# An encoder layer in fp32 on one core: x transposed ahead of the modulation rows, and g1, sh2, sc2 summed on VectorE during the projections

## The chip, the cores and the metric

The kernel runs on one core of a Trainium2 chip. The metric is the time of one execution on the device, in microseconds (us). TensorE multiplies matrices, VectorE and ScalarE work on elements and read its results out of PSUM, GpSimd is a slower helper, SyncE issues most of the loads. The profile calls them PE, DVE, ACT, POOL and SP.

## The reference

One layer (512 tokens, width 1024), then a mixture of experts. The parts that the change touches are the modulation and what comes before and around the four input projections:

```python
c_act = jax.nn.silu(c)
mod = (c_act @ w_mod[l] + b_mod[l])[:, None, :]
sh1, sc1, g1, sh2, sc2, g2 = jnp.split(mod, 6, axis=-1)
h = rms_norm(x) * (1.0 + sc1) + sh1
z = h @ w_in[l]
u_pool, q, k, v, g, r_f, r_b = jnp.split(z, split_at, axis=-1)
y_pool = pool_mixer(u_pool, w_pool[l], pool_scale[l])
y_gla = gla_mixer(q, k, v, g, r_f, r_b, w_gk_up[l], b_gk[l], gla_norm_g[l])
mix = jnp.concatenate([y_pool, y_gla], axis=-1) @ w_out[l]
x = x + g1 * mix
h = rms_norm(x) * (1.0 + sc2) + sh2
x = x + g2 * moe_ffn(h, w_router, b_router, w1[l], w3[l], w2[l])
return rms_norm(x) * final_g
```

c is one row of 1024 numbers, w_mod is 1024 x 6144, so mod is one row of 6144 numbers and costs a read of 25 MB. The result is float32; the projections are computed as three products of high and low parts.

## The kernel before

Everything is written out by hand: each engine has its own program, and they meet at semaphores. The order of the code is the order on each engine.

**Loads.** The ring has 8 slots of 2 MB. Until the experts begin, SyncE uses slots 0 to 3 in turn (STREAM): m0 to m3, u, qk, v, g, m4 to m11, wo0, wo1. "m" units are 512 columns of w_mod, u, qk, v, g those of w_in, wo those of w_out. Each load waits until the slot's last unit is used up. Slots 6 and 7 hold scratch (scr) in this phase: q, k, v, the pooling input `up`, the rows of the first modulation numbers (modr).

**TensorE's jobs.** JOBS is the list of results in PSUM, in TensorE's order. Job number j takes bank j % 8, and start() makes TensorE wait until job j - 8 has been read out, by ScalarE (OUT_SCALAR) or VectorE (OUT_VECTOR), each in its own order.

**Modulation.** mod_rows(i) multiplies c, spread to 32 columns (cb), by the unit m_i in four column groups of the array: 8 products (line 532), each in two instructions. For m0 to m3 (sh1, sc1) ScalarE copies the result (mr0 to mr3) to modr, and 16 small products with `sel` (line 545) turn it into columns (mcol), to which VectorE adds the bias (modc). For m4 to m11 (g1, sh2, sc2, g2) mod_pair spreads the row over all partitions by a product with `sel` (line 635, jobs mb4 to mb11), and VectorE adds a bias that GpSimd loads as a broadcast over 128 partitions (bias_b, line 1684, issued after g3).

**Start.** ScalarE sums squares of x, VectorE makes xn, and TensorE, after mcol, transposes it in 32 transposes (line 551, xT0 to xT7). ScalarE scales and shifts each (line 1074), VectorE splits it in h_hi and h_lo.

**Projections.** product() runs over 8 chunks k of a unit; for each, ScalarE writes w_hi (line 1067), VectorE w_lo (line 1297), in DEPTH = 4 buffers, and TensorE does 12 products (line 572). The order is u, r (low_rank), q and k, gk (line 619), v, yp (line 625, the pooling's map), g. Meanwhile GpSimd does the pooling windows of u (lines 1674 to 1681), ScalarE and VectorE the gates: from gk comes the negative absolute value (neg_abs), then exp, ln (softplus), then a scan over each chunk (lines 1321 to 1325). Their place in VectorE's program is fixed between low_weights(20, 24) and low_weights(24, 28).

**Attention and output.** After g: the decays on ScalarE (line 1116), decayed(i) on VectorE (lines 1338 to 1341), the products att, the mask copies (line 1375), the transposes kdt, the products upd, the states (lines 1392 and 1395), the products o (lines 686 and 698), and the output projection wo0, wo1 with the norms. Then the second norm, the router, and 16 pairs of experts.

Of the kernel before, what the change touches and what calls it, by code (L numbers as in the profile page):

```python
# [25 lines left out]
F32 = mybir.dt.float32  # L26
# [7 lines left out]
P = 128  # L34
D = 1024
S = 512
# [31 lines left out]
CP = dict(ident=(0, 128), iota=(128, 192), off=(192, 200), tok=(200, 204))  # L68
CP_N = 204
# [19 lines left out]
def constants():  # L89
# [6 lines left out]
    cp[:, 200:204] = r[:, None] + P * np.arange(NT)[None] - S  # L96
    ct = np.zeros((P, CT_N), np.float32)
# [11 lines left out]
    for w, (_, _, ed) in zip(WINDOWS, POOL_AT):  # L109
# [9 lines left out]
JOBS = ([f"mr{i}" for i in range(4)] + ["mcol"] + [f"xT{k}" for k in range(KD)]  # L119
        + [f"u{i}" for i in range(4)] + ["r", "q0", "q1", "k0", "k1"] + [f"gk{i}" for i in range(4)]  # L120
        + [f"v{i}" for i in range(4)] + [f"yp{i}" for i in range(4)] + [f"g{i}" for i in range(4)]
        + [f"m{a}{i + j}" for i in (4, 6) for a in "rb" for j in range(2)]
        + [f"att{d}{h}" for d in range(2) for h in range(HEADS)]
        + [f"kdt{d}{p}" for d in range(2) for p in range(2)]
        + [f"m{a}{8 + j}" for a in "rb" for j in range(2)]
        + [f"upd{d}{p}{par}" for d in range(2) for p in range(2) for par in range(2)]
        + [f"m{a}{10 + j}" for a in "rb" for j in range(2)]
# [6 lines left out]
STREAM = (["m0", "m1", "m2", "m3", "u", "qk", "v", "g"] + [f"m{i}" for i in range(4, 12)] + ["wo0", "wo1"])  # L134
SU = {n: i for i, n in enumerate(STREAM)}
PRE_UNITS = len(STREAM)
# [5 lines left out]
OUT_SCALAR = ([f"mr{i}" for i in range(4)] + [f"xT{k}" for k in range(KD)]  # L142
              + [f"u{i}" for i in range(4)] + ["r", "q0", "q1", "k0", "k1"] + [f"gk{i}" for i in range(4)]
              + [f"yp{i}" for i in range(4)] + [f"g{i}" for i in range(4)]
              + [f"mr{i}" for i in range(4, 8)]
              + [f"kdt{d}{p}" for d in range(2) for p in range(2)]
              + [f"mr{i}" for i in range(8, 12)] + [f"o{h}" for h in range(HEADS)]
              + [f"hT{t}{hf}" for t in range(NT) for hf in range(2)] + ["lg"])
OUT_VECTOR = (["mcol"] + [f"v{i}" for i in range(4)] + [f"mb{i}" for i in range(4, 8)]
              + [f"att{d}{h}" for d in range(2) for h in range(HEADS)] + ["mb8", "mb9"]  # L150
              + [f"upd{d}{p}{par}" for d in range(2) for p in range(2) for par in range(2)]
              + ["mb10", "mb11"] + [f"rb{h}" for h in range(HEADS)]
# [3 lines left out]
PRE_USES = [len(range(i, PRE_UNITS, PRE_SLOTS)) if i < PRE_SLOTS else 0 for i in range(SLOTS)]  # L156


def build(nc, A, out, g2_row, x1_row):
    ctx = ExitStack()  # L160
    with ctx:
# [29 lines left out]
        h_hi = place("h_hi", BIG, [P, KD, S], F32R)  # L191
# [172 lines left out]
        def unit(slot, k):  # L364
            return ring[:, slot, :].rearrange("p (k n) -> p k n", k=k)
# [68 lines left out]
        def _(sp):  # L434
# [4 lines left out]
            for n in range(PRE_UNITS):  # L439
                slot = n % PRE_SLOTS  # L440
                if n >= PRE_SLOTS:
                    used_up(sp, n - PRE_SLOTS)
# [1301 lines left out]
```

## Time and profile before

| what | value |
|---|---|
| median of 3 runs | 794.06 us (788.34, 796.72, 794.06) |
| profiled execution | 791.07 us, span 789.2 us |
| TensorE busy, share of the span | 706.9 us, 90% |
| VectorE busy | 300.2 us, 38% |
| ScalarE busy | 175.5 us, 22% |
| GpSimd busy | 46.6 us, 6% |
| mean granted TensorE clock | 0.950 of full speed |
| end of the first output projection's second half (wo13) | 244.6 us |

The span runs from the first to the last instruction; 1.9 us lie around it. The work named above fills the first 245 us; the router and the experts fill the rest.

### The profile page before, as it was taken

The numbers are of one execution on the slowest core, as the hardware profiler recorded it, in microseconds if no ns is written. First come the engines' busy times: TensorE is split into PE (matmuls) and PEld (weight loads), VectorE is DVE, ScalarE is ACT, GpSimd is POOL, SyncE is SP. The second block draws the span as 40 slices with busy tenths as digits, with TensorE's granted clock in tenths as the row PEclk, the third lists the DMA queues.
The fourth block names the chain that finished last, engine by engine and source line by source line (L and its number), as shares of the span: only waits on it lengthen the run. The fifth ranks groups of instructions, "written<-read, shape, count | busy, mean of one in ns | idle before, by whom it ended". The sixth has DMA issues, their size and how long they took to land.

```text
span 789.2 us, 9101 instructions
## 1 busy us (share of the span) xinstructions
PE 706.9 (90%) x3786; PEld 382.4 (48%) x3786; DVE 300.2 (38%) x565; ACT 175.5 (22%) x308; POOL 46.6 (6%) x50
## 2 busy tenths in 40 slices
PE   1899999989998289999877999999999998998994
PEld 0388787457686234443333434434443453453442
DVE  1081354177685602333304233333333333322326
ACT  3153363514335012101110101102111110110104
POOL 0004700000000000000000000000000000000000
PEclk9789999999999579999986999999999999999998
DMA  9983330797226939999997799999999999999972
GB/s 338 387 321 108 107 106 6 299 387 285 92 108 229 425 123 432 424 429 397 426 417 310 289 404 428 428 426 423 429 428 425 426 425 429 426 427 426 427 312 106
DMA packets 38857, 261.22 MB, mean 331 GB/s; under 512 B 4002, under 2 KB 4386, under 8 KB 26016
## 3 DMA queue, kind: packets, MB, share of 16 engines
q1 hardware_dynamic: 34560, 250.64, 77.4%
q0 software_dynamic: 2480, 6.16, 2.1%
q10 hardware_dynamic: 1776, 3.84, 1.3%
q8 instruction: 31, 0.51, 0.3%
q14 instruction: 10, 0.08, 0.0%
HBM read 260.76 MB, written 4.20 MB: 336 GB/s over the span
## 4 chain that ended last, share of the span: by engine, by line
PE 73%; DMA 19%; DVE 5%; ACT 2%; issue 1%; SPq 1%; DVEq 0%; ACTq 0%; POOLq 0%
PE bank L841 23%; PE bank L572 17%; DMA ring<-in_w 12%; PE bank L850 12%; PE bank L858 3%; PE bank L859 2%; DMA x_rows<-mid 2%; PE bank L532 2%; DMA ring<-in_w_mod 2%; PE bank L815 2%; PE bank L830 1%; DVE x L1549 1%; DMA xg_rows<-x_rows,keep 1%; DMA after<-in_b_mod 1%; PE bank L833 1%
## 5 line engine op out<-in xcount | busy, mean ns | idle before, releaser
L841 PE MATMUL bank<-ring,low 128*64 128x512 f32 x1024 | 230.0, 603 | 12.3 <-DMA ring<-in_w 9.7
L841 PEld LDWEIGHTS bank<-ring,low 128*64 128x64 f32 x1024 | 77.2, 139 | 155.3 <-issue 155.3
L1549 DVE TENSOR_TENSOR x<-x,bank 128x512 f32<-128x512 f32 x136 | 84.4, 682 | 84.5 <-PE bank L859 82.7
L850 PE MATMUL bank<-ring,low 128*64 128x512 f32 x512 | 113.4, 595 | 0.9 <-DVE x L1549 0.9
L850 PEld LDWEIGHTS bank<-ring,low 128*64 128x64 f32 x512 | 36.2, 137 | 66.1 <-issue 64.4
L1539 DVE SCALAR_TENSOR_TENSOR y_raw<-bank,keep,g2b 128x512 f32<-128x512 f32 x32 | 24.0, 751 | 88.4 <-PE bank L850 88.4
L858 PE MATMUL bank<-y_hi,slot_tok 128*128 128x512 f32 x128 | 53.8, 420 | 0.2 <-DVE y_lo L1544 0.2
L1599 DVE TENSOR_TENSOR low<-low,bank 128x512 f32<-128x512 f32 x16 | 11.0, 689 | 112.7 <-PE bank L841 112.7
L859 PE MATMUL bank<-y_lo,slot_tok 128*128 128x512 f32 x128 | 50.6, 395 | 0.0
L1228 ACT COPY low<-bank 128x512 f32<-128x512 f32 x16 | 9.4, 586 | 175.8 <-PE bank L823 175.8
L532 PE MATMUL bank<-ring,low 128*32 128x512 f32 x192 | 28.6, 737 | 18.0 <-DMA ring<-in_w_mod 17.8
L1236 ACT CAST y_hi<-y_raw 128x512 fp32r<-128x512 f32 x32 | 19.8, 618 | 105.5 <-DVE y_raw L1539 105.5
L1699 POOL DMA_INDIRECT xg_rows<-x_rows,keep x16 | 15.9, 997 | 441.4 <-PE bank L815 396.4
L1297 DVE TENSOR_TENSOR w_lo<-ring,w_hi 128x512 fp32r<-128x512 f32 x32 | 22.9, 727 | 45.7 <-ACT w_hi L1067 45.7
L858 PEld LDWEIGHTS bank<-y_hi,slot_tok 128*128 128x128 f32 x128 | 24.0, 187 | 30.0 <-issue 25.2
L572 PE MATMUL bank<-h_hi,w_hi 128*128 128x512 f32 x96 | 37.9, 394 | 0.0
L572 PE MATMUL bank<-h_hi,w_lo 128*128 128x512 f32 x96 | 37.4, 390 | 0.0
L572 PE MATMUL bank<-h_lo,w_hi 128*128 128x512 f32 x96 | 37.4, 390 | 0.0
L1226 ACT ACTIVATE low<-bank 128x512 f32<-128x512 f32 x16 | 9.6, 597 | 101.1 <-PE bank L841 101.1
L1544 DVE TENSOR_TENSOR y_lo<-y_raw,y_hi 128x512 fp32r<-128x512 f32 x32 | 22.2, 693 | 21.9 <-ACT y_hi L1236 21.9
L1067 ACT CAST w_hi<-ring 128x512 fp32r<-128x512 f32 x32 | 19.7, 619 | 46.4 <-PE bank L572 46.4
L859 PEld LDWEIGHTS bank<-y_lo,slot_tok 128*128 128x128 f32 x128 | 24.1, 188 | 4.3
(245 smaller groups left out, 802.9 us busy)
## 6 DMA issues: line engine op xcount, KB each, us to landing
ring<-in_w SPq DMA_DIRECT2D x99, 2048.0 KB, 20.5
ring<-in_w_mod SPq DMA_DIRECT2D x12, 2048.0 KB, 15.2
ring<-in_w_in SPq DMA_DIRECT2D x4, 2048.0 KB, 21.1
ring<-in_w_out SPq DMA_DIRECT2D x2, 2048.0 KB, 12.9
x<-in_x SPq DMA_DIRECT2D x4, 512.0 KB, 6.7
after<-in_b_mod POOLq DMA_DIRECT2D x1, 2048.0 KB, 8.1
x_rows<-mid ACTq DMA_DIRECT2D x4, 512.0 KB, 11.6
out<-x SPq DMA_DIRECT2D x4, 512.0 KB, 2.7
```

What stands on the lines that cost most here:

```text
L532: last = mm(b[32 * j:32 * j + 32, :], cb[:, k, :], w[:, k, :], start=k < 4, stop=k >= 4, tile_position=(0, 32 * j), skip_group_check=True)
L572: last = mm(out_, lhs, rhs, start=k == 0 and n == 0, stop=stop and n == 2)
L841: last = mm(bk[e * CAP:(e + 1) * CAP, :], xb[:, k, e * CAP:(e + 1) * CAP], unit(n % SLOTS, KD)[:, k, :], start=k == 0, stop=k == KD - 1)
L850: last = mm(bk[e * CAP:(e + 1) * CAP, :], hid_t[:, k, e * CAP:(e + 1) * CAP], unit(n % SLOTS, KF)[:, k, hf * 512:(hf + 1) * 512], start=k ...
L858: mm(bk[:, :], slot_tok[:, buf, t * P:(t + 1) * P], hi[:, c], start=True, stop=False)
L859: return mm(bk[:, :], slot_tok[:, buf, t * P:(t + 1) * P], lo[:, c], start=False, stop=True)
L1067: nc.scalar.copy(w_hi[:, c % DEPTH, :], raw_chunk(c)).then_inc(w_hi_ready, 1)
L1236: nc.scalar.copy(y_hi[:, c], y_raw[:, c]).then_inc(yh_ready, 1)
L1297: v.tensor_tensor(lo, raw_chunk(c), hi.bitcast(F32), ALU.subtract).then_inc(w_lo_ready, 1)
L1539: return v.scalar_tensor_tensor(raw[:, c], (Y0, Y1)[hf][:, :], w_slot[:, buf:buf + 1], g2b[:, c], ALU.mult, ALU.mult)
L1544: return v.tensor_tensor(lo[:, c], raw[:, c], hi[:, c].bitcast(F32), ALU.subtract)
L1549: return v.tensor_tensor(acc[:, t, c], acc[:, t, c], bk[:, :], ALU.add)
```

## The change

**Start.** The transposes stand first on TensorE (xT0 to xT3, then xT4 and xT5, xT6 and xT7 between the modulation rows). VectorE copies them raw to h_raw, and ScalarE scales and shifts them in place (mixed) once its half of the columns is there: mcol0 comes from m0 and m2, mcol1 from m1 and m3. The loads come as m0, m2, u, m1, m3, qk, and m1, m3 and mcol1 are computed inside the u product (h_part, before chunks 2, 3 and 4). The square root is taken for each tile of x. The `sel` constants load later, since the small products now use one column (quarter) of the constants that come first.

**g1, sh2, sc2.** The units m4 to m9 are no longer multiplied on TensorE. VectorE adds w_mod's 8 row blocks of each, scaled by c, into mod_sum[i], 8 steps for a unit, 48 in all, two after each low part from chunk 8 on (mod_steps). GpSimd clears the sums and puts the bias in one of their rows. A product with ones then sums over partitions and spreads at once (mod_spread, 6 products), and ScalarE reads it out (mod_out). m4 goes to `mid`, m5 to slot 6. Only m10 and m11 (g2) remain as rows; the broadcast load of the bias is gone.

```diff
-JOBS = ([f"mr{i}" for i in range(4)] + ["mcol"] + [f"xT{k}" for k in range(KD)]
+JOBS = ([f"xT{k}" for k in range(4)] + ["mr0", "xT4", "xT5", "mr2", "xT6", "xT7", "mcol0", "mr1", "mr3", "mcol1"]
         + [f"u{i}" for i in range(4)] + ["r", "q0", "q1", "k0", "k1"] + [f"gk{i}" for i in range(4)]
-        + [f"v{i}" for i in range(4)] + [f"yp{i}" for i in range(4)] + [f"g{i}" for i in range(4)]
-        + [f"m{a}{i + j}" for i in (4, 6) for a in "rb" for j in range(2)]
+        + ["mb4", "mb5"] + [f"v{i}" for i in range(4)] + ["mb6", "mb7"]
+        + [f"yp{i}" for i in range(4)] + [f"g{i}" for i in range(4)]
+        + ["mr10", "mr11", "mb8", "mb9", "mb10", "mb11"]
...
+MIDDLE = SLOTS
+STREAM = dict(m0=0, m2=1, u=2, m1=3, m3=0, qk=1, m4=MIDDLE, m5=6, v=3, g=0, m6=2, m7=1, m8=2, m9=1, m10=2, m11=3,
+              wo0=1, wo1=0)
...
+            def h_part(k):
+
+                if k == 2:
+                    mod_rows(1, later_rows[1])
+                elif k == 3:
+                    mod_columns(later_columns, 1)
+                    mod_rows(3, later_rows[3])
+                elif k == 4:
+                    mod_columns(later_columns, 3).then_inc(job_done, 1)
+                pe.wait_ge(h_parts, k + 1)
...
+            def mod_spread(i):
+
+                b = start(f"mb{i}")
+                pe.wait_ge(mod_summed, KD * (i - 3))
+                mm(b[:, :], ones, mod_sum[i - 4], start=True, stop=True).then_inc(job_done, 1)
...
+            mod_spread(4)
+            mod_spread(5)
             product("v", [f"v{i}" for i in range(4)], h_hi, h_lo, False)
+            mod_spread(6)
+            mod_spread(7)
...
-            mod_pair(4)
-            mod_pair(6)
+            mod_rows(10)
+            mod_rows(11)
+            mod_spread(8)
+            mod_spread(9)
...
-            mod_pair(8)
             read_out(pe, "v3")
...
-            mod_pair(10)
...
-            for i in range(4):
-                decays(i)
-                mod_part(4 + i)
+            decays(0)
+            mod_part(10)
+            mod_part(11)
+            decays(1)
+            mod_out(8)
+            mod_out(9)
+            decays(2)
+            decays(3)
...
+            def mod_steps(n0, n1):
+
+                for n in range(n0, n1):
+                    i, k = divmod(n, KD)
+                    slot = STREAM[SUMMED[i]]
+                    if k == 0:
+                        dve.wait_ge(landed[slot], 16 * arrival(SUMMED[i]))
+                        dve.wait_ge(bias_in[i], 16)
+                    else:
+                        dve.wait_ge(mod_summed, n)
+                    v.scalar_tensor_tensor(mod_sum[i], unit(slot, KD)[:, k, :], cs[:, k:k + 1], mod_sum[i],
+                                           ALU.mult, ALU.add).then_inc(mod_summed, 1)
+
+            def low_weights_and_mods(c0, c1):
+
+                for c in range(c0, c1):
+                    low_weights(c, c + 1)
+                    mod_steps(2 * (c - KD), 2 * (c - KD) + 2)
+
+            low_weights_and_mods(8, 20)
...
-            low_weights(24, 28)
+            low_weights_and_mods(24, 28)
             for t in range(NT):
                 b = full(dve, f"v{t}")
                 v.tensor_copy(v_s[:, t, :], b[:, :]).then_inc(out_vector, 1)
...
-            dve.wait_ge(bias_in, 16)
-            decayed(0)
-            decayed(1)
-            mod_row(4)
-            mod_row(5)
-            decayed(2)
-            decayed(3)
-            mod_row(6)
-            mod_row(7)
+            for i in range(4):
+                decayed(i)
+            dve.wait_ge(g2bias_in, 16)
+            mod_row(10)
+            mod_row(11)
...
-            pool.dma_start(bias_b, A["b_mod"][:, 2 * D:6 * D].to_broadcast([P, 4 * D])).then_inc(bias_in, 16)
+            pool.dma_start(g2bias, A["b_mod"][:, 5 * D:6 * D]).then_inc(g2bias_in, 16)
```

**Place 1, TensorE at the start.** Before, from its first product; line 532 is mod_rows, 545 the small products, 551 the transposes:

```order
L532 MATMUL bank<-ring,low 32x512 [waits landed0,cb_ready]
L532 MATMUL bank<-ring,low 32x512 x7
L532 MATMUL bank<-ring,low 32x512 [waits landed1]
...
L545 MATMUL bank<-ring 128x1 [waits out_scalar,tmp_in]
...
L532 MATMUL bank<-ring,low 32x512 [waits landed2]
...
L532 MATMUL bank<-ring,low 32x512 [waits landed3]
...
L551 MATMUL bank<-keep,mid 128x128 [waits ident_in,xn_ready]
```

Now, up to the first product of u; line 550 is mod_rows, 557 the small products, 562 the transposes, 598 the products:

```order
L562 MATMUL bank<-keep,mid 128x128 [waits ident_in,xn_ready]
L562 MATMUL bank<-keep,mid 128x128 x15
L550 MATMUL bank<-ring,low 32x512 [waits landed0,cb_ready]
L550 MATMUL bank<-ring,low 32x512 x7
L562 MATMUL bank<-keep,mid 128x128 x8
L550 MATMUL bank<-ring,low 32x512 [waits landed1]
...
L557 MATMUL bank<-keep,ring 128x1 [waits out_vector,out_scalar]
L557 MATMUL bank<-keep,ring 128x1 x3
...
L557 MATMUL bank<-keep,ring 128x1 [waits out_scalar]
...
L598 MATMUL bank<-h_hi,w_hi 128x512 [waits w_lo_ready,w_hi_ready,h_parts,out_vector,out_scalar]
```

Half of the rows and of the small products now stand before the u product, with all the transposes between them; the other half went behind its second chunk.

**Place 2, TensorE between v and g.** The four products yp (line 625 before), each of which takes the bank of the job eight before it:

```order
L625 MATMUL bank<-ring,low 128x512 [waits pooled,out_scalar] x4
```

Now, the two spreads mb6 and mb7 (line 642) and the same four products (line 662):

```order
L642 MATMUL bank<-low,ring 128x512 [waits mod_summed,out_scalar] x2
L662 MATMUL bank<-ring,low 128x512 [waits pooled,out_scalar] x2
L662 MATMUL bank<-ring,low 128x512 [waits pooled,out_vector] x2
```

The last two of yp moved from banks that ScalarE reads out (gk2, gk3) to banks that VectorE reads out (v0, v1).

**Place 3, VectorE between the gates and g.** Before, from the last gate's scan (lines 1321 and 1325) over the low parts of g's first chunks (1297) to the copies of v (1330):

```order
L1321 SCALAR_TENSOR_TENSOR mid<-mid 128x512 [waits softplus]
L1325 SCALAR_TENSOR_TENSOR mid<-ring,mid 128x512 [waits vector_chain]
L1297 TENSOR_TENSOR w_lo<-ring,w_hi 128x512 [waits w_hi_ready] x4
L1330 COPY ring<-bank 128x512 [waits job_done] x4
L1297 TENSOR_TENSOR w_lo<-ring,w_hi 128x512 [waits w_hi_ready] x4
```

Now (low parts 1361, mod_steps 1394, copies of v 1423):

```order
L1414 SCALAR_TENSOR_TENSOR mid<-mid 128x512 [waits softplus]
L1418 SCALAR_TENSOR_TENSOR mid<-ring,mid 128x512 [waits vector_chain]
L1361 TENSOR_TENSOR w_lo<-ring,w_hi 128x512 [waits w_hi_ready]
L1394 SCALAR_TENSOR_TENSOR ring<-ring,keep 128x512 [waits bias_in4,landed2]
L1394 SCALAR_TENSOR_TENSOR ring<-ring,keep 128x512 [waits mod_summed]
...
L1423 COPY ring<-bank 128x512 [waits job_done] x4
```

Eight steps of the sums now stand among the four low parts, ahead of the copies of v.

## Rows read from the trace of the kernel before

**Rows 1.** The chain that ended last, in order of time: start us, us, what.

```profile
3.99 17.37 DMA ring<-in_w_mod
...
39.47 6.43 PE bank L551 x32
45.91 48.98 PE bank L572 x216
94.88 3.63 PE bank L619 x8
...
123.94 21.82 PE bank L572 x96
...
146.39 8.08 DMA after<-in_b_mod
...
239.16 5.48 PE bank L572 x24
```

**Rows 2.** Timeline of TensorE: start us, us, engine, line, op, tiles, idle before.

```profile
16.09 3.64 PE L532 MATMUL bank<-ring,low 128*32 128x512 f32 x16 [16.09 <-DMA ring<-in_w_mod]
...
25.79 1.92 PE L545 MATMUL bank<-ring 128*128 128x1 f32 x16 [0.81 <-ACT ring L1047]
...
169.44 3.64 PE L532 MATMUL bank<-ring,low 128*32 128x512 f32 x32
...
184.29 0.61 PE L686 MATMUL bank<-ring 128*128 128x128 f32 x4
...
196.73 0.50 PE L572 MATMUL bank<-wo_hi,pool_hi 128*128 128x512 f32 x1
```

**Rows 3.** Windows: stretch, busy us of each engine, PEclk (granted clock), DMA share, GB/s.

```profile
28.00:32.00 4.00, 3.31 (x19) 0.88 (x11) 0.00 (x0) 0.58 (x1) 0.00 (x0) 0.52 1.05 386
164.00:166.00 2.00, 1.00 (x9) 1.03 (x11) 2.00 (x4) 0.00 (x0) 0.84 (x1) 0.68 1.05 386
166.00:168.00 2.00, 2.00 (x16) 1.78 (x14) 2.00 (x5) 0.00 (x0) 0.00 (x0) 0.50 1.05 388
168.00:170.00 2.00, 2.00 (x21) 1.53 (x23) 1.90 (x4) 1.84 (x4) 0.00 (x0) 0.97 1.05 385
```

**Rows 4.** Timeline of VectorE, from the start to the g product.

```profile
13.56 2.74 DVE L1285 TENSOR_SCALAR mid<-x,keep 128x1024 f32<-128x1024 f32 x4
...
39.72 1.67 DVE L1288 TENSOR_SCALAR keep<-keep 128x8 f32<-128x8 f32 x1
...
98.10 2.50 DVE L1315 SCALAR_TENSOR_TENSOR mid<-mid 128x512 f32<-128x512 f32 x4 [1.84 <-ACT mid L1093]
...
113.07 1.22 DVE L1323 TENSOR_TENSOR_SCAN mid<-ring,mid 128x512 f32<-128x512 f32 x1
...
119.74 2.47 DVE L1297 TENSOR_TENSOR w_lo<-ring,w_hi 128x512 fp32r<-128x512 f32 x4
122.13 2.48 DVE L1330 COPY ring<-bank 128x512 f32<-128x512 f32 x4
```

**Rows 5.** Timeline of VectorE after the g product.

```profile
154.70 0.69 DVE L1338 TENSOR_TENSOR big<-big,ring 128x512 f32<-128x512 f32 x1 [18.44 <-DMA after<-in_b_mod]
...
176.19 0.29 DVE L1392 COPY mid<-bank 128x128 f32<-128x128 f32 x1 [0.47 <-PE bank L671]
...
184.22 2.33 DVE L1395 SCALAR_TENSOR_TENSOR big<-big,keep,bank 128x128 f32<-128x128 f32 x6
```

**Rows 6.** Timeline of ScalarE: the softplus and the first decays.

```profile
111.60 2.20 ACT L1101 ACTIVATE mid<-mid 128x512 f32<-128x512 f32 x4
...
148.75 0.20 ACT L1119 ACTIVATE keep<-mid 128x8 f32<-128x8 f32 x1
```

**Rows 7.** Timeline of VectorE, one low part while GpSimd works.

```profile
79.25 1.22 DVE L1297 TENSOR_TENSOR w_lo<-ring,w_hi 128x512 fp32r<-128x512 f32 x1 [1.66 <-ACT w_hi L1067]
```

**Rows 8.** Timeline of GpSimd, two sums of the pooling windows.

```profile
78.87 1.05 POOL L1674 TENSOR_TENSOR spread<-ring 128x518 f32<-128x518 f32 x1
80.00 1.37 POOL L1674 TENSOR_TENSOR ring<-spread 128x516 f32<-128x516 f32 x1
```

More of the change, by code:

```diff
@@ L198, in build @@
         wo_hi = place("wo_hi", 4 * UNIT, [P, KD, 512], F32R)
-        wo_lo = [place(f"wo_lo{hf}", SU[f"wo{hf}"] % PRE_SLOTS * UNIT, [P, KD, 512], F32R) for hf in range(2)]
+        wo_lo = [place(f"wo_lo{hf}", STREAM[f"wo{hf}"] * UNIT, [P, KD, 512], F32R) for hf in range(2)]
         wr_hi = place("wr_hi", LOW, [P, KD, P], F32R)
@@ L277, in build @@
         base = (base + 15) // 16 * 16
+        last_sum = scr[:, base:base + 512]
+        base += 512
         assert base <= 2 * UNIT
+        mod_sum = [last_sum] + [low[:, i * 512:(i + 1) * 512] for i in range(3)] + [rst, last_sum]
         route = place("route", BIG + D, [P, 2 * D])
@@ L438, in _ @@
                 sp.dma_start(x1[:, t, :], x_r[:, t, :]).then_inc(x_in[t], 16)
[L439 to L442, printed above, removed]
-                sp.dma_start(unit(slot, KD), pre_source(n)).then_inc(landed[slot], 16)
+            for name, slot in STREAM.items():
+                if arrival(name) > 1:
+                    used_up(sp, [n for n in NAMES if STREAM[n] == slot][arrival(name) - 2])
+                elif slot == MIDDLE:
+                    sp.wait_ge(job_done, JOB["xT7"] + 1)
+                sp.dma_start(unit(slot, KD), pre_source(name)).then_inc(landed[slot], 16)
             def expert_unit(n):
@@ L534, in mod_rows, with mod_columns, x_transposed @@
                 last.then_inc(job_done, 1)
-            pe.wait_ge(cb_ready, 1)
-            columns = bank[JOB["mcol"] % 8]
-            assert JOB["mcol"] < 8
-            def mod_columns(i0, i1):
-                read_out(pe, f"mr{i1 // 4 - 1}")
-                for i in range(i0, i1):
-                    last = mm(columns[:, i:i + 1], modr[:, i * P:(i + 1) * P], sel[:, 0:1], start=True, stop=True)
-                return last
-            def x_transposed(k):
-                b = start(f"xT{k}")
+            def mod_columns(b, i):
+                read_out(pe, f"mr{i}")
+                for j in range(4 * i, 4 * i + 4):
+                    last = mm(b[:, j:j + 1], modr[:, j * P:(j + 1) * P], quarter, start=True, stop=True)
+                return last
+            def x_transposed(k, b):
                 for t in range(NT):
@@ L1093, in _, with mod_out @@
                 a(la[:, i // 2, i % 2, :], b[:, :], ACT.Identity, bias=col["bgk"][:, i:i + 1]).then_inc(out_scalar, 1)
+            def mod_out(i):
+                b = full(act, f"mb{i}")
+                dst = (g1b, sh2b, sc2b)[(i - 4) // 2][:, (i % 2) * 512:(i % 2 + 1) * 512]
+                a(dst, b[:, :], ACT.Identity, bias=1.0 if i > 7 else 0.0).then_inc(out_scalar, 1)
+            mod_out(4)
+            mod_out(5)
             high_parts(20, 22)
@@ L1134, in _ @@
                 nc.scalar.copy(kdtok[:, i // 2, i % 2, :, :].rearrange("p t c -> p (t c)"), b[:, :]).then_inc(out_scalar, 1)
-            for i in range(8, 12):
-                mod_part(i)
             def high_cat(k):
@@ L1682, in _ @@
                 pool.wait_ge(pooled, g + 1)
+                if g == 0:
+                    pool.wait_ge(job_done, JOB["r"] + 1)
+                    link(g_.memset(low[:, 0:3 * 512], 0.0))
+                    for i in range(1, 4):
+                        bias_row(i)
+            link(g_.memset(mod_sum[4], 0.0))
+            bias_row(4)
+            pool.wait_ge(job_done, JOB["mb4"] + 1)
+            link(g_.memset(mod_sum[5], 0.0))
+            bias_row(5)
             pool.wait_ge(job_done, JOB["g3"] + 1)
-            pool.dma_start(bias_b, A["b_mod"][:, 2 * D:6 * D].to_broadcast([P, 4 * D])).then_inc(bias_in, 16)
+            pool.dma_start(g2bias, A["b_mod"][:, 5 * D:6 * D]).then_inc(g2bias_in, 16)
             pool.wait_ge(qe_ready, 4)
```

234 lines of the change are left out of this document (131 added, 103 removed).

## The prediction

> **What bounds the kernel now.** I read the chain of waits first, because TensorE's 90% busy share mixes stages with different limits. For the first 245 us the chain is TensorE's own work, nearly without gaps: the projections from 45.9 us on, with 96 products of 0.227 us for a unit, that is 21.8 us [rows 1]. It leaves TensorE in three places that the change touches. Up to 45.9 us it waits for the first loads and then goes through the modulation rows, 3.64 us each, the small products, and 32 transposes of 6.43 us [rows 1, 2]. After the last product of g (145.8 us; I call it G) it goes to the broadcast load of the bias, 8.08 us, and from there to VectorE, which begins the decayed parts at 154.7 us [rows 1, 5]. And between 169 and 185 us it passes rows and spreads of the modulation on TensorE [rows 2]. From the end of wo13 (244.6 us, [rows 1]) to the end the loads of the experts start, in both kernels, from the same events: slots 2, 3 and one more are filled before, five after. So I take that part as moved whole, 0 us.
>
> The last view is the granted clock. It stood at 0.52 of 2.4 GHz from 28 to 32 us, while TensorE did rows and small products, and at 0.50 (1.2 GHz) at 166 to 168 us, after the waits for VectorE ahead of it; it had come back by 168 to 170 us (0.97) [rows 3]. That stretch cost 2 x (0.32 + 0.50 + 0.03) = 1.7 us of dense work. I take 1.7 us as the least price of a wait of some microseconds, and twice that as the most.
>
> **The start.** With its square root per tile, xn is ready somewhat earlier than the 16.3 us of before [rows 4]; I take 15.5 us. Sixteen transposes at the low clock take 3.2 us (half of 6.43), to 18.7. The row of m0 takes 3.64 us at the low clock and 1.82 at the full one (3.64 for two, [rows 2]); the clock should rise during it, so 2.75. Then, at full clock, 0.9 + 1.8 + 0.96 + 0.9 + 0.96 us for transposes, the row of m2, and the small products (1.92 us for 16 instructions, [rows 2]): 27.0 us. The loads don't hold this up: a unit takes 2.1 MB / 388 GB/s = 5.4 us [rows 3], m0 arrives some 1.2 us earlier since `sel` no longer loads ahead of it, so u is there at about 25.7. From mcol0 over VectorE, ScalarE and VectorE to the first product I count 3.1 us (the same steps took 2.6 us without the column sum). The u product starts at 30.1 us instead of 45.9. But it now contains two rows and two sets of small products, 2 x (1.82 + 0.96) = 5.5 us; a wait for the same chain behind mcol1, 3.4 us (GpSimd's clearing of `up` still starts there, as when the column step took 1.67 us, [rows 4]); and two times of low clock, after these two waits, for which I take 2 and 1 us. End of u: 30.1 + 21.8 + 5.5 + 3.4 + 3 = 63.8, against 45.9 + 21.8 = 67.7: **-3.9 us**. Bounds: -7.6 us if the clock never falls, and +1 us if everything ahead of u runs at the low clock (17.4 instead of 11.5 us) and the rest as above.
>
> **What TensorE does more between u and g.** Four spreads: mb4 and mb5 after gk, mb6 and mb7 after v. Four products of that kind (gk) take 3.63 us [rows 1], and the spreads lie on TensorE's path: **+3.4 us**, with little doubt.
>
> **VectorE in the projections.** A step with one more operand takes 2.50 / 4 = 0.62 us in a row of four [rows 4], a little more when it waits for the step before; a low part 2.47 / 4 = 0.62. So a chunk costs VectorE 1.95 us instead of 0.62, and TensorE needs 2.72 us for it. In q and k, where nothing else stands on VectorE, this is hidden. It isn't in v. Let V be the start of the v product (94.9 + 3.6 = 98.5 before). Softplus's first part is there at V + 13.8 [rows 6] in both kernels; VectorE, with two low parts and four steps behind the exponentials, is free at V + 14.3. Then follow the four gates with their scans, 7.4 us (112.3 to 119.7, where [rows 4] has the first scan and what comes after), four low parts with their eight steps, 7.8 us, and only then the copy of v0, read out at V + 30.1. Before, the eight steps weren't there, the copies ran from 122.1 to 124.6 [rows 4] and g began at 123.9 [rows 1]: the cover was already down to nothing. TensorE wants v0's bank for the third yp product, at V + 22.0 + 4 x 0.86 = V + 25.4. It waits **+4.7 us** (3.5 to 7, by how much the steps' own waits add). Behind it the clock falls, for two slow yp products and the first of g: **+2.5 us** (1.7 to 3.4). These 7 us are on the path: the yp copies on ScalarE, its high parts of g and all of g on TensorE queue behind that product.
>
> **After g.** Gone: the load of 8.08 us, four rows and their four spreads ahead of the attention, and two more pairs later. ScalarE's first decays were there at G + 3.1 us (148.95, [rows 6]), and nothing now keeps VectorE from starting there instead of at G + 8.9. Its four parts follow ScalarE (2.1 us apart, with copies and read-outs between) to G + 11.6; the two rows of g2 1.3 us, to 12.9, where GpSimd's clearing of att also ends; the eight mask copies 5 us, to G + 18; then the states, which took 176.19 to 186.55 = 10.4 us [rows 5]. Before they began at G + 30.4. The products o can begin when three quarters of the states are there: G + 25.7; they take 196.73 - 184.29 = 12.4 us up to wo0 [rows 2]. TensorE has now idled for 5 us and more ahead of them, so I add 2.2 us of low clock, and 1 us because transposes and upd may also run at the low clock. wo0 starts at G + 41.3, before at G + 50.9: **-9.6 us** (-12.4 without any low clock, -8 with all of it). g2 is saved long before ScalarE's wo parts need it, and wo0 lies in its slot by then.
>
> **Sum.** -3.9 + 3.4 + 4.7 + 2.5 - 9.6 = -2.9 us, made against the profiled 791.07: 788.2 us. The median of the three runs lies 3.0 us above the profiled one, so I expect **791.2 us**.
>
> **Rival 1: no wait before g.** If the steps are cheaper beside their neighbours than I think, or the softplus comes early enough, VectorE reads v0 out in time and the clock stays up. Against it stands that before the change there was no slack between 122.1 and 123.9. The terms 4.7 and 2.5 vanish: -10.1 us, 784.0 us.
>
> **Rival 2, slower: VectorE falls behind while GpSimd pools.** A low part that began at 79.25 took 1.22 us instead of 0.69; it ended 0.55 us after GpSimd's sum that ran to 79.92, and the next sum took 1.37 us instead of 1.05 [rows 7, 8]. They kept each other out. Now three such instructions stand in each chunk of q and k. If each waits for a sum of 1.05 us, a chunk takes 3 x (0.62 + 1.05) = 5.0 us, eight of them lag by 18 us, the four buffers cover 10.9, and TensorE waits 7.3 us there; what is left of the lag delays gates and v copies by some 4 us more. That gives -2.9 + 11.3 = +8.4, 802.5 us. It decides where the mean wait passes (2.72 - 1.95) / 3 = 0.26 us. Against it: GpSimd's scaling steps don't seem to block, VectorE can catch up during them, and the pooling ends before v is half done. The Trainium skill ("SBUF — State Buffer", Who interferes with whom) has the rule: a VectorE instruction with two SBUF inputs and a GpSimd instruction that reads SBUF take turns, each blocked for the whole of the other. By that rule, the trace agrees, and the new steps are all of that kind, so it speaks against this change, by up to the sum above.
>
> **Rival 3: the early transposes bring nothing.** The clock stays low up to the u product: +1 in place of -3.9, 796.1 us.
>
> A page has one more thing to say on the clock. The Trainium skill ("TensorE: Matmul & The Clock Gate", The HAM clock gate) calls the low clock the default, which activity lifts. By that the transposes at 15.5 us, which keep TensorE busy without a pause, are a good place to begin; the rows of before, with pauses for loads, were a worse one. It would favour the forecast over rival 3.
>
> **Chances.** Forecast 0.60, rival 1 0.22, rival 2 0.12, rival 3 0.06. About 1% (7.9 us) is what a measurement of this kernel can tell from no change. Faster by over 1%: rival 1 and a bit of the forecast, 0.24. Slower: rival 2, 0.12. Within 1%: 0.64. The range takes in the forecast's bounds and half of rival 1, and leaves rival 2 out: 784 to 800 us.
>
> **What would show it.** First product of u near 30 us, last near 64. TensorE idle for some 5 us at the third yp product, released by VectorE's copy of v, with a granted clock under 1 behind it. Low parts in q and k at about 0.8 us with no idle time of TensorE there. First decayed part 3 us after g, o some 26 us after it, wo13 at about 241.7. I am wrong if TensorE waits for low parts or for sums in q, k or v, if a load of m6 to m9 holds VectorE up, or if the stretch behind wo13 doesn't keep its 544.6 us.

## The result, and the profile after

The changed kernel takes 802.41 us (median of four runs, 799.28 to 805.20) against 792.18 us of the kernel before (median of four, 788.34 to 796.72): ratio 1.0145, 95% interval 1.0107 to 1.0183. It is slower by 10 us where I forecast 791.2, and the time lies outside my range of 784 to 800. The profiled execution took 799.28 us, span 797.2, mean granted clock 0.936 (before 0.950).

The chain of waits shows where the stages end. Its columns are start, duration and what ran.

```profile
27.79 8.21 PE bank L598 x24
...
50.17 12.77 PE bank L598 x48
...
131.13 22.30 PE bank L598 x96
...
202.73 5.02 PE bank L598 x12
...
246.87 5.48 PE bank L598 x24
```

These answer to [rows 1, 2]. The u product now ends at 50.17 + 12.77 = 62.9 us, before at 67.6: 4.7 us gained. The g product ends at 131.13 + 22.30 = 153.4, before at 145.8: 7.7 us lost. And wo13 ends at 252.35 against 244.6: still 7.7 us lost. What follows wo13 is 797.2 - 252.35 = 544.9 us, 544.6 before. So two things have to be found: what costs 12.4 us between the ends of u and g, and where the 9.6 us are that I expected to win behind g.

TensorE's timeline has both places. In brackets stands the idle time ahead and what ended it.

```profile
127.36 3.78 PE L662 MATMUL bank<-ring,low 128*128 128x512 f32 x4 [6.45 <-DVE ring L1423]
...
166.18 2.08 PE L682 MATMUL bank<-big 64*128 64x128 f32 x16 [2.64 <-DVE after L1442]
...
170.76 3.72 PE L704 MATMUL bank<-ring,mid 64*64 64x128 f32 x128
179.97 1.20 PE L717 MATMUL bank<-ring 128*128 128x128 f32 x4 [5.48 <-DVE big L1477]
```

The wait of 6.45 us ahead of the third yp product is the one I had forecast at 4.7, and L1423 is the copy of v0. In VectorE's timeline one sees why the copy is late: four low parts with eight sums (those of m8) stand between the scans and it. This answers to [rows 4], where four low parts without sums stood ahead of the copy, and to [rows 5].

```profile
117.30 1.22 DVE L1418 TENSOR_TENSOR_SCAN mid<-ring,mid 128x512 f32<-128x512 f32 x1
118.44 0.67 DVE L1361 TENSOR_TENSOR w_lo<-ring,w_hi 128x512 fp32r<-128x512 f32 x1
119.02 1.53 DVE L1394 SCALAR_TENSOR_TENSOR ring<-ring,keep 128x512 f32<-128x512 f32 x2
...
125.17 1.53 DVE L1394 SCALAR_TENSOR_TENSOR ring<-ring,keep 128x512 f32<-128x512 f32 x2
126.62 2.47 DVE L1423 COPY ring<-bank 128x512 f32<-128x512 f32 x4
156.75 0.69 DVE L1431 TENSOR_TENSOR big<-big,ring 128x512 f32<-128x512 f32 x1 [11.38 <-ACT keep L1175]
...
172.03 0.29 DVE L1474 COPY mid<-bank 128x128 f32<-128x128 f32 x1 [0.95 <-PE bank L704]
```

Behind g VectorE does what I expected of it: the decayed parts begin at 156.75, that is G + 3.3, and o can start at 179.97, G + 26.5 (forecast 25.7, before G + 38.5). What went wrong is o itself. The windows, which answer to [rows 3], give busy time of PE, PEld, DVE, ACT and POOL, then the granted clock:

```profile
128.00:130.00 2.00, 2.00 (x3) 0.67 (x2) 1.09 (x2) 0.54 (x1) 0.00 (x0) 0.50 0.94 289
...
178.00:180.00 2.00, 0.04 (x1) 0.07 (x1) 1.79 (x6) 0.88 (x2) 0.00 (x0) 0.96 0.76 315
180.00:182.00 2.00, 2.00 (x12) 1.77 (x14) 1.76 (x6) 0.00 (x0) 0.00 (x0) 0.50 0.08 25
...
190.00:196.00 6.00, 6.00 (x42) 5.32 (x42) 0.00 (x0) 2.24 (x4) 0.00 (x0) 0.50 0.00 0
...
206.00:208.00 2.00, 2.00 (x10) 1.19 (x12) 0.00 (x0) 0.30 (x1) 0.00 (x0) 0.71 0.00 0
```

TensorE is busy without a pause from 180 us on, and yet its clock stays at 0.50 (1.2 GHz) until 206, the whole of o and the first chunk of wo0. o took 202.73 - 179.97 = 22.8 us instead of 12.4 [rows 2], the first twelve wo products 5.02 us instead of 12 x 0.227 = 2.7. In the kernel before, the same stretches ran at full clock; there the last rows and spreads of the modulation stood directly ahead of o:

```profile
182.00:184.00 2.00, 2.00 (x12) 0.62 (x4) 1.76 (x6) 1.39 (x3) 0.00 (x0) 1.00 1.04 385
184.00:186.00 2.00, 2.00 (x21) 1.71 (x20) 1.82 (x6) 1.26 (x3) 0.00 (x0) 1.00 0.88 322
```

### The profile page after: what moved, and what is told of

It is laid out like the page before. It is cut to its first block, busy times and chain, and to the rows that moved or that the text cites. A ratio compares the mean times of both kernels' runs of the same rounds, so it can differ in the third digit from the quotient of the medians.

```text
span 797.2 us, 8972 instructions
## 1 busy us (share of the span) xinstructions
PE 704.2 (88%) x3690; PEld 389.6 (49%) x3690; DVE 345.4 (43%) x620; ACT 175.5 (22%) x311; POOL 58.7 (7%) x60
## 4 chain that ended last, share of the span: by engine, by line
PE 65%; DMA 18%; DVE 12%; ACT 2%; issue 2%; POOL 1%; SPq 0%; DVEq 0%; POOLq 0%
PE bank L872 23%; PE bank L598 12%; DMA ring<-in_w 12%; PE bank L881 11%; PE bank L889 3%; DVE low L1394 3%; PE bank L890 2%; DMA x_rows<-mid 2%; DMA ring<-in_w_mod 2%; DVE w_lo L1361 2%; PE bank L729 2%; PE bank L846 2%; PE bank L861 1%; DMA xg_rows<-x_rows,keep 1%; DVE x L1629 1%
## 5 line engine op out<-in xcount | busy, mean ns | idle before, releaser
L1795 POOL DMA_INDIRECT xg_rows<-x_rows,keep x16 | 15.9, 997 | 441.7 <-PE bank L846 398.1
L598 PE MATMUL bank<-h_hi,w_hi 128*128 128x512 f32 x96 | 40.7, 424 | 6.2 <-DVE w_lo L1361 3.3
L598 PE MATMUL bank<-h_hi,w_lo 128*128 128x512 f32 x96 | 39.2, 408 | 0.0
L598 PE MATMUL bank<-h_lo,w_hi 128*128 128x512 f32 x96 | 39.0, 406 | 0.0
L1361 DVE TENSOR_TENSOR w_lo<-ring,w_hi 128x512 fp32r<-128x512 f32 x32 | 27.8, 871 | 20.9 <-ACT w_hi L1091 20.9
L598 PEld LDWEIGHTS bank<-h_hi,w_hi 128*128 128x128 f32 x96 | 19.4, 202 | 12.6 <-issue 5.5
## 6 DMA issues: line engine op xcount, KB each, us to landing
x_rows<-mid ACTq DMA_DIRECT2D x4, 512.0 KB, 11.1
```

The costliest lines, as they stand in the source:

```text
L598: last = mm(out_, lhs, rhs, start=k == 0 and n == 0, stop=stop and n == 2)
L1361: v.tensor_tensor(lo, raw_chunk(c), hi.bitcast(F32), ALU.subtract).then_inc(w_lo_ready, 1)
```

## The experiments

Theory A has two parts. The clock: TensorE stands still for 5.5 us ahead of o, its clock falls, and o cannot raise it. The queue: m8's sums ahead of the copies of v make the wait ahead of g. The rivals: o is slow for another reason than its clock; what one place gains another gives back; or GpSimd's work beside VectorE's sums is the cause. A saving below is the difference between a run's median and the changed kernel's 802.4 us. The medians of the kernel before beside these runs were 792.14, 791.76 and 792.90 us, so it moved by about 1 us; the changed kernel's own median is known only to some 3 us either way (the interval above).

**Products ahead of o (e1_products_ahead_of_o).**

```diff
                 read_out(pe, "att13")
+                for _ in range(6 if pr == 0 else 0):
+                    mm(b[0][:, :], ones, reset, start=True, stop=True)
                 read_out(pe, f"upd1{pr}1")
```

> The changed kernel with six products more of ones (128x128) with a 128x512 tile of float32, put on TensorE between the last update product (174.6 us) and the first o product (180.0), into the bank of o0, which the first o products overwrite. They take 0.86 us each at the full clock, 5.2 in all, and fit into the 5.5 us in which TensorE waited for the states. Theory A (o is slow because TensorE stood still ahead of it and its clock fell, and o's small products don't raise it again): granted clock 1.00 over o, o in 12 to 13 us instead of 22.8, the first twelve wo products in 2.7 instead of 5.0, the time 12 to 13 us shorter, 789 to 791. Theory B (the clock matters little, o is slow for the states or their semaphores, or because its operands are read while another engine writes): o stays near 22 us and the time at 800 to 803, or up to 2 us longer.

Measured: 791.32 us (ratio to before 0.9975, 0.9950 to 1.0000), 11.1 us saved by work that computes nothing. The windows of this run over the gap and o:

```profile
178.00:180.00 2.00, 2.00 (x7) 0.80 (x6) 1.75 (x7) 2.00 (x5) 0.00 (x0) 1.00 0.98 422
180.00:182.00 2.00, 2.00 (x8) 0.99 (x7) 1.79 (x6) 0.59 (x2) 0.00 (x0) 1.00 0.63 262
182.00:184.00 2.00, 2.00 (x25) 1.69 (x24) 1.75 (x6) 0.00 (x0) 0.00 (x0) 1.00 0.04 8
184.00:190.00 6.00, 6.00 (x74) 5.25 (x72) 4.91 (x9) 2.02 (x4) 0.00 (x0) 1.00 0.00 0
```

The clock is 1.00, and the first wo product follows the first o product by 194.16 - 181.71 = 12.45 us. In 184 to 190 us, 74 of o's matrix instructions are done; the changed kernel does 42 in six us. States, semaphores and operands are the same in both, so theory B of this run is out: the clock is the whole of the 10 us that o took longer.

**The kernel before without its cover (e4_before_without_m10_m11).** In the kernel before, the last mod_pair's work is cut to one column for each product; g2 is left out.

```diff
-            mod_pair(10)
+            for j in (10, 11):
+                b = start(f"mr{j}")
+                slot_in(f"m{j}")
+                mm(b[:, 0:1], sel, sel[:, 0:1], start=True, stop=True).then_inc(job_done, 1)
+            for j in (10, 11):
+                b = start(f"mb{j}")
+                read_out(pe, f"mr{j}")
+                mm(b[:, 0:1], sel, mrow[:, j % 2, 0:1], start=True, stop=True).then_inc(job_done, 1)
```

> The kernel before with the products of m10 and m11 ahead of o cut from whole tiles to one column each, so g2 is left out of the computation; everything else as in the kernel before. It is less work for TensorE, which then stands still some 4 to 5 us before o as in the changed kernel. Theory A: the granted clock falls to 0.50 over o, o takes 20 to 23 us instead of 12.3, and the time is 8 to 13 us longer than before though work was taken away, 800 to 805. Theory B (those products only cost their time): the same or up to 4 us shorter, 788 to 792, with o at a clock of 1.00.

Measured: 805.53 us against 792.14, ratio 1.0152 (1.0120 to 1.0183). Taking two rows (1.8 us each) and two spreads (0.9 each) from TensorE made the kernel before 13.4 us slower, which is as slow as the changed one. In the profiled pair the loads happened to let u begin 2.5 us earlier in this run (43.4 against 45.9 us), and wo13 still ended 8.5 us later (253.2 against 244.6). Its TensorE timeline, and then its windows, show the same fall of the clock as the changed kernel's, here without any single long stand: two of less than 2 us, with next to no work between them, were enough.

```profile
176.54 0.61 PE L679 MATMUL bank<-ring 128*128 128x1 f32 x4 [0.26 <-DVE mid L1402]
179.11 0.80 PE L683 MATMUL bank<-after,ring 128*128 128x1 f32 x4 [1.96 <-DVE mid L1402]
181.77 1.20 PE L693 MATMUL bank<-ring 128*128 128x128 f32 x4 [1.86 <-DVE big L1402]
```

```profile
178.00:180.00 2.00, 0.80 (x4) 0.72 (x4) 1.79 (x6) 2.00 (x5) 0.00 (x0) 0.85 1.02 371
180.00:182.00 2.00, 0.23 (x1) 0.26 (x2) 1.75 (x7) 0.11 (x1) 0.00 (x0) 0.50 1.06 389
182.00:184.00 2.00, 2.00 (x14) 1.77 (x16) 1.75 (x6) 0.00 (x0) 0.00 (x0) 0.50 0.70 258
...
196.00:202.00 6.00, 6.00 (x41) 5.32 (x41) 0.00 (x0) 0.00 (x0) 0.00 (x0) 0.50 0.47 202
```

o went from 181.77 to 204.46: 22.7 us. So rows and spreads that I had booked as pure cost, and their removal as a gain, had carried the clock of what came next.

**How much cover (e8_two_products_ahead_of_o).** As the first run, with `range(2 if pr == 0 else 0)`.

> As the run with six products ahead of o, with two of them: 1.7 us of work and then some 3.5 us of standing still. It asks how much cover the clock wants. If it falls only for a long stand: o at 1.00, 12.5 us, 789 to 792. If any gap of this size is enough: o as slow as in the changed kernel, 20 to 23 us, 800 to 804. Between them the clock falls a little later or comes back during o.

Measured: 802.13 us (two runs; ratio 1.0128, 1.0070 to 1.0187), nothing saved. The two products end at 178.7, then TensorE stands still for 3.13 us, and the clock falls from 1.00 to 0.50 after o has begun:

```profile
180.00:182.00 2.00, 0.16 (x1) 0.16 (x2) 1.77 (x6) 0.85 (x2) 0.00 (x0) 1.00 0.70 299
182.00:184.00 2.00, 2.00 (x17) 1.76 (x17) 1.74 (x5) 0.00 (x0) 0.00 (x0) 0.63 0.11 41
184.00:186.00 2.00, 2.00 (x14) 1.77 (x14) 2.00 (x4) 0.00 (x0) 0.00 (x0) 0.50 0.00 0
```

It did not come back before o's end at 204.04. A stand of 3 us here costs what one of 5.5 us costs.

**m8 behind the copies of v (e2_m8_behind_v).**

```diff
-            low_weights_and_mods(24, 28)
+            low_weights(24, 28)
             for t in range(NT):
                 b = full(dve, f"v{t}")
                 v.tensor_copy(v_s[:, t, :], b[:, :]).then_inc(out_vector, 1)
+            mod_steps(32, 40)
             low_weights_and_mods(28, 32)
```

> The changed kernel with VectorE's order altered at one place: the four low parts of g's first chunks stand without sums between them, then the four copies of v, then the eight sums of m8, then the rest as it was. Nothing is left out. Theory A (the 6.5 us in which TensorE waits for the first copy of v are VectorE's queue alone, 8 sums of 0.77 us ahead of it): first v copy at about 121 instead of 126.6 us, TensorE's wait 0.7 instead of 6.5, the clock ahead of g at 1.00, end of g 6 to 8 us earlier, and the time 6 to 9 us shorter, 794 to 796. Theory B (what g gains is given back, because the sums then hold up the decayed parts or g's low parts): end of g 3 or less earlier, or the first decayed part at the same place as now, 156.8, and the time 800 to 803.

Measured: 794.51 us (ratio to before 1.0028, 1.0004 to 1.0053), 7.9 us saved. TensorE's timeline of this run:

```profile
121.89 1.98 PE L662 MATMUL bank<-ring,low 128*128 128x512 f32 x4 [0.66 <-DVE ring L1423]
```

The wait fell from 6.45 to 0.66 us, and these two products (four instructions) from 3.78 to 1.98. The wait was the queue, and its follow-on cost is seen by comparing the stretch from the third yp product to the end of g: 153.43 - 127.36 = 26.1 us in the changed kernel, 145.68 - 121.89 = 23.8 here, 2.3 us for the clock. o still took 22.7 us.

**No sums (e3_no_sums).**

```diff
-                    v.scalar_tensor_tensor(mod_sum[i], unit(slot, KD)[:, k, :], cs[:, k:k + 1], mod_sum[i],
-                                           ALU.mult, ALU.add).then_inc(mod_summed, 1)
+                    dve.sem_inc(mod_summed, 1)
```

> The changed kernel without the 48 summing steps of VectorE: the semaphore is counted up without them, so g1, sh2 and sc2 are left out of the computation. Theory A (two separate losses: VectorE's sums make the wait ahead of g, the gap ahead of o makes the low clock over o): TensorE's wait ahead of g is gone, the end of g 8 to 9 us earlier, but o still starts behind 4 to 6 us of standing still and takes 20 to 23 us at a granted clock near 0.50; 791 to 795 in all. Theory B (all the loss comes from VectorE's load beside GpSimd): o is fast again as well, 778 to 783.

Measured: 769.34 us, shorter than either theory. But wo13 ended at 244.2 us, where the run with m8 moved had it at 243.7; the rest, 522 us instead of 545, is the experts' part, which runs on other values once g1, sh2 and sc2 are missing. I take that for the reason, which isn't shown, and don't compare the totals. What can be compared is the part ahead: o took 22.7 us, from 171.87 to 194.57, and at 0.50, so VectorE's load isn't what slows it. And leaving out all 48 sums gained no more than moving the eight of m8. The other 40 cost nothing that shows on the path: from the end of u to the end of wo13 the two runs differ by 0.1 us.

**GpSimd's pooling left out (e10_no_pooling_on_gpsimd).** One scaling of one column stands in for the sums of each group; yp is left out of the computation.

```diff
-                while m < w:
...
-                    link(g_.tensor_tensor(to, src[:, 0:n], src[:, m:m + n], ALU.add))
...
-                g_.tensor_tensor(u, src[:, 0:S], u, ALU.subtract).then_inc(pooled, 1)
+                u = up[:, o + left:o + left + 1]
+                g_.tensor_scalar(u, u, 1.0 / w, None, ALU.mult).then_inc(pooled, 1)
```

> The changed kernel with the pooling sums of GpSimd left out: one scaling of one column for each group stands in for them, so yp is not what the reference has. It asks what part of the wait ahead of g is GpSimd's work beside VectorE's sums (the rival of the prediction). If the two engines delay each other: VectorE's sums and low parts between 73 and 100 us take 0.77 and 0.69 us as elsewhere instead of 1.09 and 1.35 on average, the scans may start up to 4 us earlier and the first v copy at 122 to 125 instead of 126.6. If they only queue: their times are as in the changed kernel, and so is the 6.5 us wait. By the theory that the eight sums of m8 make the wait, 4.5 us or more of it stay either way.

Measured: 848.1 us in all (one run), of which 593 us lie behind wo13, where other values reach the experts again; not comparable. wo13 ended at 252.7, as in the changed kernel (252.35). VectorE's groups between 73 and 101 us (busy, mean ns, idle before), first of the changed kernel:

```profile
L1394 DVE SCALAR_TENSOR_TENSOR low<-ring,keep,low 128x512 f32<-128x512 f32 x16 | 17.5, 1094 | 0.5 <-DMA low<-in_b_mod 0.3
L1361 DVE TENSOR_TENSOR w_lo<-ring,w_hi 128x512 fp32r<-128x512 f32 x8 | 11.4, 1428 | 5.6 <-ACT w_hi L1091 5.6
```

and of this run:

```profile
L1394 DVE SCALAR_TENSOR_TENSOR low<-ring,keep,low 128x512 f32<-128x512 f32 x16 | 12.0, 749 | 2.4 <-DMA low<-in_b_mod 2.2
L1361 DVE TENSOR_TENSOR w_lo<-ring,w_hi 128x512 fp32r<-128x512 f32 x8 | 5.5, 690 | 6.7 <-ACT w_hi L1091 6.6
```

So the two engines do hold each other up: 17.5 + 11.4 - 12.0 - 5.5 = 11.4 us of VectorE's time, a low part taking 1.43 us beside GpSimd and 0.69 without it. The Trainium skill ("SBUF — State Buffer", Who interferes with whom) says that such instructions of the two take turns; the trace agrees. Nearly all of it stays off the path, but not the last 1.1 us. In the changed kernel VectorE has no idle time from 76 us up to the copies of v. The low part that stands behind the exponentials begins at 106.94, though ScalarE had its high part ready at 105.8. Without GpSimd's work VectorE is early there and waits for that high part instead. First the changed kernel, then this run:

```profile
106.94 0.68 DVE L1361 TENSOR_TENSOR w_lo<-ring,w_hi 128x512 fp32r<-128x512 f32 x1
...
107.19 0.69 DVE L1361 TENSOR_TENSOR w_lo<-ring,w_hi 128x512 fp32r<-128x512 f32 x1 [1.87 <-ACT w_hi L1091]
```

Only 0.3 us of this can be seen in the first v copy, which came at 126.86 (126.62 in the changed kernel), 31.2 us behind the start of the v product at 95.66 (31.5 behind 95.10). The reason is TensorE's clock, which in this run stood at 0.50 when v began (94 to 96 us), so that ScalarE's first high part in v came 4.2 us behind the start of v instead of 3.4. The wait ahead of g was 5.36 us here; in the run with products of v and att moved (e5, below), which has GpSimd's work and the same fall of the clock at the start of v, it was 5.37. From the 1.1 us of VectorE's lateness I estimate GpSimd's share of the 6.45 us at about 1 us; no run shows it by itself.

**The place of four spreads (e6_spreads_back_ahead_of_o).** The jobs and their read-outs move along in the tables, ScalarE's read-outs of mb8 and mb9 and VectorE's two g2 rows in the programs.

```diff
             mod_rows(10)
             mod_rows(11)
-            mod_spread(8)
-            mod_spread(9)
-            for j in (10, 11):
...
+            mod_spread(8)
+            mod_spread(9)
+            for j in (10, 11):
...
             for pr in range(2):
                 b = [start(f"o{2 * pr + hh}") for hh in range(2)]
```

> The changed kernel with the spreads of m8 and m9 and of the two g2 rows (four products, 0.86 us each at the full clock) put back where the kernel before had its last pair, between the update products and o; the rows of m10 and m11 stay behind g. Nothing is left out and nothing added: one part of the change, the place of these four, is undone. They leave the path ahead of the decayed parts (VectorE's two g2 rows, 1.27 us, too) and fill 3.4 of the 5.5 us gap. Theory A: the masks start some 1.3 us earlier, the granted clock is 1.00 over o, o takes 12.5 us and the first wo products 2.7; in all 12 to 15 us off, 787 to 790. Theory B (the cover has to be of work that takes the whole gap): the clock falls for the 2 us that are left, o takes over 18 us, 795 to 801.

Measured: 790.82 us (ratio to before 0.9991, 0.9963 to 1.0020), 11.6 us saved with the same work. TensorE's timeline of this run:

```profile
177.68 1.98 PE L709 MATMUL bank<-after,ring 128*128 128x512 f32 x4 [0.59 <-DVE mid L1475]
180.55 0.68 PE L718 MATMUL bank<-ring 128*128 128x128 f32 x4 [0.88 <-DVE big L1475]
```

Pauses of 0.59 and 0.88 us are left, the clock is 1.00 from 172 us to the end of o, and o took 12.5 us. The smaller part of my expectation failed: the masks did not start 1.3 us earlier, since VectorE then waited 1.17 us for GpSimd's clearing of att in place of the two g2 rows.

**A part of o into the gap (e5_products_with_v_first).** All products of v and att stand ahead of the wait for the backward states. They are 16, in 32 of the 144 matrix instructions of o.

```diff
+            read_out(pe, "att13")
+            o_banks = []
+            for h in range(HEADS):
+                o_banks.append(start(f"o{h}"))
+                for t in range(NT):
+                    mm(o_banks[h][:, t * P:(t + 1) * P], v_s[:, t, h * DV:(h + 1) * DV], att[:, h, t * P:(t + 1) * P],
+                       start=t == 0, stop=False, skip_group_check=True)
             for pr in range(2):
-                b = [start(f"o{2 * pr + hh}") for hh in range(2)]
-                read_out(pe, "att13")
+                b = o_banks[2 * pr:2 * pr + 2]
                 read_out(pe, f"upd1{pr}1")
                 for t in range(NT):
-                    for hh in range(2):
...
```

Only the first product into a bank has start=True. The Trainium skill ("PSUM — Partial Sum Buffer", PSUM: the matmul accumulator) says that such a product clears the marks by which the bank tells adding from overwriting; with start=True in each t, the later ones would make the products with the states overwrite. No run here shows that case.

> The changed kernel with the 32 products of v and att (half of what o is) taken out of the loop over o and put ahead of the wait for the backward states; the products with the states follow as before. Nothing is left out. They need only the banks of o, which come free as the forward states are read out (174.9 and 177.2 us), and at the full clock take some 4.5 us of o's 12.4 (128x128 products, 0.61 us for four that overlap). Theory A: TensorE is busy in most of the 5.5 us gap, its clock holds, and o behind the gap is 8 us; first wo product at 188 instead of 202.7, the time 786 to 789. Theory A2: the products keep TensorE busy but, being small, don't hold the clock: o's second half at 0.50 takes some 14 us, the time 792 to 796. Theory B (the gap is the states' chain alone and the order is unimportant): 800 to 803.

Measured: 786.54 us (ratio to before 0.9913, 0.9879 to 0.9947), 15.9 us saved. Its TensorE timeline and two windows:

```profile
175.56 2.02 PE L715 MATMUL bank<-ring 128*128 128x128 f32 x16 [0.35 <-DVE mid L1481]
178.04 2.05 PE L715 MATMUL bank<-ring 128*128 128x128 f32 x16 [0.46 <-DVE mid L1481]
180.61 0.44 PE L732 MATMUL bank<-big 64*128 64x64 f32 x4 [0.52 <-DVE big L1481]
```

```profile
182.00:184.00 2.00, 2.00 (x40) 2.00 (x40) 1.86 (x5) 0.02 (x1) 0.00 (x0) 1.00 0.00 0
184.00:186.00 2.00, 2.00 (x40) 2.00 (x40) 2.00 (x4) 2.00 (x4) 0.00 (x0) 1.00 0.00 0
```

No pause is longer than 0.52 us, and the rest of o, 64-row products alone, stays at 1.00 and ends at 187.0, 6.4 us after it began.

**Both repairs (e7_spreads_back_and_m8_behind_v, e9_v_first_and_m8_behind_v).** The edits are those above, put together.

> The two repairs together: the eight sums of m8 behind the copies of v, and the four spreads back between the update products and o. Nothing is left out. If the two losses are separate (theory A), they add: 8 and 13 us off the changed kernel, 779 to 783, which is 9 to 13 us below the kernel before. If they share a cause or one exposes a further wait (theory B, g's low parts or wo's high parts come late), 786 to 792.

> The changed kernel with the two rearrangements that showed most: the products of v and att ahead of the wait for the backward states, and the eight sums of m8 behind the copies of v. Nothing is left out. Apart they took 15.9 and 7.9 us off the changed kernel's median of 802.4. If they add: 777 to 781, the shortest of all here. If the earlier g only lets a further wait show (wo's high and low parts late, the clock not held): 782 to 787.

Measured: 781.71 us (ratio to before 0.9875, 0.9830 to 0.9921), 20.7 us saved where the single runs give 11.6 + 7.9 = 19.5; and 776.94 us (0.9808, 0.9764 to 0.9852), 25.5 saved where they give 15.9 + 7.9 = 23.8. The two losses are separate and add up. The last one beats the kernel before by 16 us (792.90 beside it). In its TensorE timeline both waits are small:

```profile
122.41 1.99 PE L662 MATMUL bank<-ring,low 128*128 128x512 f32 x4 [0.66 <-DVE ring L1427]
...
166.84 2.02 PE L715 MATMUL bank<-ring 128*128 128x128 f32 x16
169.32 2.20 PE L715 MATMUL bank<-ring 128*128 128x128 f32 x16 [0.45 <-DVE mid L1482]
171.88 0.44 PE L732 MATMUL bank<-big 64*128 64x64 f32 x4 [0.37 <-DVE big L1482]
```

and wo13 ends at 226.2 us, 18.4 before the kernel before.

## Why the prediction was wrong, step by step

By the trace the sum up to wo13 should have been -2.9 us and is +7.7, 10.6 us off.

- **The start.** Forecast -3.9, measured -4.7. The first u product came at 27.8 (forecast 30.1). How exact this is depends on the loads: in the run on the kernel before without m10 and m11, which is unchanged up to there, u began at 43.4 us instead of 45.9, and in the variants of the changed kernel it began at 27.8 to 28.9. So the miss of 0.8 us is within what the loads do, and the gain itself is known to some 2.5 us only. The bound of -7.6 doesn't come out of its terms: without the 3 us of low clock the sum is -6.9.
- **The spreads.** Forecast +3.4. What is left of the end of g after the other terms is 7.7 + 4.7 - 6.45 - 2.3 = 3.6 us. Right.
- **The wait ahead of g.** Forecast +4.7 (3.5 to 7), measured 6.45, inside the bounds. The mechanism was right and is shown by moving m8. V being the start of the v product, the copy of v0 was through at V + 32.2 instead of V + 30.1, and the third yp product wanted it at V + 25.8 instead of V + 25.4. Softplus wasn't the reason: its first part was there at V + 14.1 (forecast 13.8), but the scans began at V + 16.0 instead of V + 14.3, because VectorE's queue was late, 1.1 us of it from q and k, where GpSimd works beside it. The four low parts with their eight steps took 8.2 us instead of 7.8.
- **The low clock behind it.** Forecast +2.5, measured 2.3.
- **After g.** This is the step that failed: forecast -9.6, measured 0. VectorE's part was right to within 1 us (o starts at G + 26.5). I had seen that TensorE idles ahead of o, but priced it at 2.2 us, one fall of the clock and its return, from [rows 3], where dense work came back to full clock in some 4 us. It cost 10.4 us in o and 2.3 in the first wo chunk. My upper bound for the term, -8, allowed 1.6 us more, not the case in which the clock doesn't come back. (The lower one, -12.4, is the term less its 3.2 us of low clock, which makes -12.8.) With o at half clock throughout, 12.4 us in place of 2.2, the sum would have been -2.9 + 10.2 = +7.3 us, and the forecast 801.4.
- **The part behind wo13.** Forecast 544.6, measured 544.9.
- **Rival 2** gave 802.5 us and would look right by its number. It wasn't what happened: VectorE did lose 11.4 us beside GpSimd, yet TensorE never waited for a low part in q and k, and wo13 ended at the same time without GpSimd's work (252.7). Of its 11.3 us about 1 was real, inside the wait ahead of g. The low parts took 1.43 us there, not the 0.8 that I forecast for them. Rival 1 is ruled out by the 6.45 us; what it would have given is not far from the 7.9 us that moving m8 saved. Rival 3 is ruled out by the start.
- **The clock.** I had cited the Trainium skill ("TensorE: Matmul & The Clock Gate", The HAM clock gate) for the low clock as the default that activity lifts. At the start the durations agree: the first sixteen transposes took 3.59 us and the next eight 1.10, although the granted clock reads 1.00 in both stretches. For o the trace doesn't agree with "TensorE is busy" as the meaning of activity: it was busy in 6.00 of 6.00 us at a clock of 0.50.

In the run with six products ahead of o, 549.6 us passed from wo13 to the end, where the others that compute the full output have 544.6 to 547.3. Its profiled execution, 794.13 us, was the slowest of ten and 2.8 us above their median of 791.3, so most of that is the one execution. What stays open is why o's products don't raise the clock, with TensorE busy all the time, while the transposes of the attention do.

## What to carry to other kernels

Before taking work away from TensorE ahead of a stage of small products, look at whether that work held its clock: a stand of 3 us there cost 11 us, as much as one of 5.5 us, and filling it with products that compute nothing gave the 11 us back. Price a low clock by the stage that follows it: the products of 512 columns came back from it, and a stage that doesn't pays nearly twice its own time. And when sums are put into another engine's spare time, walk its queue up to each instruction that TensorE waits for; 40 of 48 were free, and the eight in front of one copy cost 8 us.

## What the runs showed of the hardware

- o's products don't raise TensorE's clock, but they keep it. At 0.50 they ran from 180 to 202 us with PE busy all the time and stayed at 0.50 (the same in five other runs); started at 1.00 they stayed at 1.00 for 12.5 us (e1, e6) and, with the 64-row ones alone, for 6.4 us (e5). The g and wo products of 512 columns raised it each time, and so did the attention products and transposes at 166 to 170 us (0.55 and 0.60, then 1.00 in the changed kernel).
- The fall comes late: after two covering products the clock still stood at 1.00 through a stand of 3.13 us, and fell to 0.50 after TensorE had taken up work again (e8).
- It doesn't need a stand. In e10 and e5 TensorE was busy in every window from 88 us on, with the last of k, the gk products (32 rows, 3.7 us), two spreads and the first of v, and the clock fell to 0.50 all the same; in the changed kernel the same stretch kept 1.00. The line is of e10:

```profile
94.00:96.00 2.00, 2.00 (x5) 0.88 (x3) 1.53 (x3) 1.33 (x3) 0.70 (x2) 0.50 0.79 284
```

- Beside GpSimd's sums, a low part of VectorE took 1.43 us on average (one in the kernel before 1.22, [rows 7, 8]) and a summing step 1.09, against 0.69 and 0.75 without them.
